# Delta-rule lengths, decays and transposes among projection blocks, norm squares added on VectorE, early modulation rows in fours, gate steps ahead of combines

## The reference, cut to what matters

```python
mod = silu(cond) @ w_ada + b_ada                  # 6 x 1024 values for each of two conditions
h = rmsnorm(x, norm_mix_w) * (1 + sc_a) + sh_a
z = h @ w_in                                      # q, k, v of the four branches, gates
q, k, v = silu(conv(z_q)), silu(conv(z_k)), silu(conv(z_v))      # the delta-rule branch
q, k = l2norm(q), l2norm(k); g = -exp(a_log) * softplus(za + dt_bias); gc = cumsum(g)
o_b = chunked delta rule over (q, k, v, gc, sigmoid(zb)), both directions, * silu(zz)
o_a, o_c, o_d = latent attention, long convolution, differential attention
x = x + gt_a * (sum_n sigmoid(z_gate_n) * (o_n @ w_branch_n)) @ w_out
h = rmsnorm(x, norm_mlp_w) * (1 + sc_m) + sh_m
x = x + gt_m * (relu(h @ w1) ** 2 @ w2)
```

## Time and profile before

| | us |
|---|---|
| median of 3 runs | 3173.61 (3170.78 to 3176.18) |
| the profiled execution, its own time | 3175.59 |
| its span | 3173.6 |
| TensorE busy / VectorE / ScalarE / GpSimd | 93% / 32% / 26% / 21% of the span |
| chain that ended last, by engine | TensorE 87%, VectorE 5%, issue 4%, ScalarE 3%, DMA 1% |

### The profile page before, as it was taken

The page is one execution under the profiler, slowest core; times in us unless marked ns, Lnnn a source line. Parts: engine busy times, 40 slices in busy tenths (PEclk is TensorE's granted clock), DMA queues, the critical chain, the costliest instruction groups (busy, mean ns, idle before and its releaser), DMA issues.

```text
span 3173.6 us, 56302 instructions
## 1 busy us (share of the span) xinstructions
PE 2953.1 (93%) x23304; PEld 2462.0 (78%) x23304; DVE 1022.6 (32%) x1984; ACT 812.6 (26%) x1218; POOL 660.2 (21%) x428
## 2 busy tenths in 40 slices
PE   6998999999999989999999898999999898999997
PEld 3557855777777889999956597567777788999996
DVE  1546613224442121111134374132344322111111
ACT  2123013222322241221231311232222214221222
POOL 0102102111112223333301110021111222333331
PEclk7999999999999999999999899999999999999999
DMA  7110011222113322223230100112221232222222
GB/s 292 34 48 8 3 36 40 77 75 75 61 66 125 111 66 90 85 92 93 93 123 27 34 3 11 51 47 75 75 71 65 84 125 83 87 92 89 85 92 73
DMA packets 56615, 234.64 MB, mean 74 GB/s; under 512 B 6624, under 2 KB 6784, under 8 KB 55136
## 3 DMA queue, kind: packets, MB, share of 16 engines
q1 hardware_dynamic: 53568, 206.67, 19.7%
q0 software_dynamic: 2848, 25.13, 2.1%
HBM read 222.96 MB, written 8.81 MB: 73 GB/s over the span
## 4 chain that ended last, share of the span: by engine, by line
PE 87%; DVE 5%; issue 4%; ACT 3%; DMA 1%; POOL 0%; SPq 0%; DVEq 0%; POOLq 0%; ACTq 0%
PE ps_dense L734 46%; PE ps_dense L727 14%; PE ps_aux L1293 3%; PE ps_dense L1242 2%; PE ps_dense L1314 2%; PE ps_aux L1039 2%; PE ps_aux L1031 2%; PE ps_aux L1019 2%; PE ps_dense L769 1%; PE ps_aux L1242 1%; PE ps_aux L756 1%; DMA w_ring<-in_w_early 1%; PE ps_dense L1305 1%; DVE att_s L2392 1%; PE ps_dense L1088 1%
## 5 line engine op out<-in xcount | busy, mean ns | idle before, releaser
L655 POOL TENSOR_TENSOR w_low<-w_ring,w_high 128x1024 fp32r<-128x1024 f32 x208 | 513.0, 2467 | 1090.1 <-ACT w_high L1547 1088.6
L734 PE MATMUL ps_dense<-h_high,w_high 128*128 128x320 f32 x2048 | 495.4, 323 | 55.6 <-DVE rs L2377 21.9
L734 PE MATMUL ps_dense<-h_low,w_high 128*128 128x320 f32 x2048 | 471.9, 312 | 0.0
L734 PE MATMUL ps_dense<-h_high,w_low 128*128 128x320 f32 x2048 | 471.8, 312 | 0.0
L727 PE MATMUL ps_dense<-h_norm,w_ring 128*128 128x512 f32 (+1 forms) x1536 | 432.8, 443 | 15.5 <-ACT h_norm L1568 7.5
L727 PEld LDWEIGHTS ps_dense<-h_norm,w_ring 128*128 128x128 f32 x1536 | 239.1, 195 | 213.7 <-issue 205.8
L734 PEld LDWEIGHTS ps_dense<-h_high,w_high 128*128 128x128 f32 x2048 | 338.6, 191 | 77.4 <-issue 61.0
L1547 ACT ACTIVATE w_high<-w_ring 128x1024 fp32r<-128x1024 f32 x208 | 218.7, 1053 | 540.2 <-PE ps_dense L734 442.8
L734 PEld LDWEIGHTS ps_dense<-h_high,w_low 128*128 128x128 f32 x2048 | 347.5, 191 | 0.0
L734 PEld LDWEIGHTS ps_dense<-h_low,w_high 128*128 128x128 f32 x2048 | 347.3, 190 | 0.0
L734 PE MATMUL ps_dense<-z_high,w_high 128*128 128x320 f32 x1280 | 296.8, 313 | 13.5 <-POOL w_low L655 13.5
(11 more groups left out here) (386 smaller groups left out, 3288.0 us busy)
## 6 DMA issues: line engine op xcount, KB each, us to landing
w_ring<-in_w_mlp SPq DMA_DIRECT2D x128, 512.0 KB, 3.7
w_ring<-in_w_gate SPq DMA_DIRECT2D x64, 640.0 KB, 3.9
w_ring<-in_w_late SPq DMA_DIRECT2D x64, 512.0 KB, 4.6
w_ring<-in_w_early SPq DMA_DIRECT2D x48, 512.0 KB, 3.7
w_ring<-in_w_in SPq DMA_DIRECT2D x48, 512.0 KB, 3.6
w_ring<-in_w_out SPq DMA_DIRECT2D x16, 512.0 KB, 3.6
arena<-in_dft POOLq DMA_DIRECT2D x2, 3264.0 KB, 12.5
par<-in_par POOLq DMA_DIRECT2D x3, 1731.0 KB, 7.4
```

The lines of the kernel that those rows point to most:

```text
L655: g.tensor_tensor(w_low[:, n % 2], ring[:, slot, 0:KC, :], w_high[:, n % 2].bitcast(F32), ALU.subtract).then_inc(w_low_in.sem, 1)
L734: last = mm(psD[:, b, s * 512:s * 512 + HALF], w_[:, par_, k, :], x_[:, k, s * HALF:(s + 1) * HALF], start=k == 0 and x_ is x_high and w_ ...
```

## The change

**Delta rule.** TensorE's list, in units of blocks: before, 8, 9, 10, cumulative sum, 11, length 0, 12, length 1, 13, lengths 2 and 3, all transposes. Now 8, 9, 10, lengths 0 and 1, 11, cumulative sum, lengths 2 and 3, 12, transposes, 13. The transposes use four PSUM banks in turn instead of two. ScalarE's squares come as soon as each silu is there, two Ln before the eviction of block 11 and two behind it, the Exp of the lengths before the decays' Exp, the last tanh behind both, and the evictions of blocks 12 and 13 each with its tanh, 12 before and 13 behind the k and v evictions. VectorE's list follows.

```diff
-                for n in range(8, 11):
-                    win_block(l, n)
...
-                for c in range(4):
-                    if c < 3:
-                        win_block(l, 11 + c)
+                win_block(l, 8)
+                win_block(l, 9)
+                win_block(l, 10)
+                length(0)
+                length(1)
+                win_block(l, 11)
+                pe.wait_ge(*g_ready.nth(l, 1))
+                pe.wait_ge(*qk_ln.nth(l, 2))
...
+                length(2)
+                length(3)
+                win_block(l, 12)
+
                 pe.wait_ge(*qk_norm.nth(l, 1))
                 for t in range(NT):
-                    if t >= 2:
-                        pe.wait_ge(*kv_tok.nth(l, t - 1))
+                    if t >= 4:
+                        pe.wait_ge(*kv_tok.nth(l, t - 3))
...
+                win_block(l, 13)
```

```diff
+            def norm_sum(l, at_end):
+                pe.wait_ge(*squares_in.nth(l, (1 + at_end) * (KC - 2)))
+                for a, b in SEGS:
+                    mm(psD[:, 0, a:b], c_("ones"), h[:, KC - 2, a:b], start=True, stop=False)
+                pe.wait_ge(*x_squared.nth(l, (2 + at_end) * KC))
+                for a, b in SEGS:
+                    last = mm(psD[:, 0, a:b], c_("ones"), h[:, KC - 1, a:b], start=False, stop=True)
...
+            def sum_squares(l, c, at_end):
+
+                n = at_end * (KC - 2) + c
+                dve.wait_ge(*x_squared.nth(l, (1 + at_end) * KC + c + 1))
+                if c > 1:
+                    dve.wait_ge(*squares_in.nth(l, n - 1))
+                v.tensor_tensor(h[:, c], h[:, c], h[:, c - 1], ALU.add).then_inc(squares_in.sem, 1)
...
-                with act.Fori(0, GROUPS - 1) as g:
+                with act.Fori(0, GROUPS - 2) as g:
                     mlp_group(l, g + 1, 0)
+                mlp_group(l, GROUPS - 1, 0, True)
...
             with act.Fori(0, DEPTH) as l:
                 chain.l, chain.n = l, 0
-                norm(l, 0)
+                root(l, 0)
```

```diff
+                at = 2 * (PACK - 1 - j)
                 for k in range(KC):
-                    last = mm(out[32 * (k % 4):32 * (k % 4) + 32], cond_pad[:, k, :], ring[:, slot, k, :],
-                              start=k < 4, stop=k >= 4)
+                    last = mm(out[32 * (k % 4):32 * (k % 4) + 32], cond_pad[:, k, at:at + 32], ring[:, slot, k, :],
+                              start=j == 0 and k < 4, stop=j == of - 1 and k >= 4, skip_group_check=True)
```

```diff
                     gate_part(l, 3 * v_ - 2)
                     row_max(v_)
+                    gate_sum(l, 3 * v_ - 2)
+                    gate_part(l, 3 * v_ - 1)
                     combine(v_)
-                    gate_part(l, 3 * v_ - 1)
                     take_values(v_ - 1)
+                    gate_sum(l, 3 * v_ - 1)
                     gate_part(l, 3 * v_)
+                    gate_sum(l, 3 * v_)
```

More of the change, by code:

```diff
@@ L910, in gdn, with length @@
             def gdn(l):
-                for n in range(8, 11):
-                    win_block(l, n)
[L915 to L920, removed]
-                for c in range(4):
-                    if c < 3:
-                        win_block(l, 11 + c)
+                def length(c):
                     pe.wait_ge(*qk_sq.nth(l, c + 1))
-                    if c == 1:
+                    if c == 3:
                         pe.wait_ge(*cum_in.nth(l, 1))
@@ L1517, in _ @@
                 pe.wait_ge(*residual.nth(l, 7))
+                norm_sum(l, 0)
+                mlp(l)
+                pe.wait_ge(*residual.nth(l, 39))
                 norm_sum(l, 1)
-                mlp(l)
-                norm_sum(l + 1, 0)
         @block.scalar
@@ L1547, in high_part, with square, squares, root @@
                 a(w_high[:, n % 2], ring[:, j, 0:KC, :], ACT.Copy).then_inc(w_high_in.sem, 1)
-            def norm(l, which):
+            def square(l, c, n):
+                act.wait_ge(*residual.nth(l, n))
+                a(h[:, c], x[:, c], ACT.Square).then_inc(x_squared.sem, 1)
+            def squares(l):
                 for c in range(KC):
-                    if which and c + 2 < N_OUT:
+                    if c + 2 < N_OUT:
                         high_part(l, B_OUT + c + 2, c + 2)
[L1553 to L1558, removed]
+                    square(l, c, c + 1)
+                mlp_high(l, 0, 0)
+                mlp_high(l, 1, 0)
+            def root(l, which):
                 act.wait_ge(*sumsq_done.nth(l, which + 1))
@@ L1642, in gdn, with gate_in @@
                 a(f8("es"), f8("es"), ACT.Exp).then_inc(cum_exp.sem, 1)
-                length_ln(l, 2)
-                length_ln(l, 3)
-                act.wait_ge(*qk_ln.nth(l, 4))
-                a(rn, rn, ACT.Exp, scale=-0.5).then_inc(qk_rs.sem, 1)
-                for c in range(2):
+                silu_tanh(l, 5)
+                def gate_in(c):
+                    act.wait_ge(*block_done.nth(l, 12 + c + 1))
+                    a(gz[:, c], psD[:, c, 0:T], ACT.Copy).then_inc(dense_out.sem, 1)
                     act.wait_ge(*dense_out.nth(l, 13 + c))
@@ L1891, in _ @@
             act.wait_ge(const_in.sem, 16)
+            for c in range(KC):
+                square(0, c, 0)
             with act.Fori(0, DEPTH) as l:
                 chain.l, chain.n = l, 0
-                norm(l, 0)
+                root(l, 0)
                 modulate(l, 0)
@@ L1902, in _ @@
                 high_part(l, B_OUT + 1, 1, 0, 3)
-                norm(l, 1)
+                squares(l)
+                root(l, 1)
                 modulate(l, 1)
@@ L1908, in _ @@
             chain.l, chain.n = DEPTH, 0
-            norm(DEPTH, 0)
+            root(DEPTH, 0)
             for c in range(KC):
```

197 lines of the change are left out of this document (117 added, 80 removed).

## The result

| | us |
|---|---|
| changed kernel, median of 4 runs | 3098.29 (3091.97 to 3102.03) |
| kernel before, median of 4 runs | 3173.23 (3170.78 to 3176.18) |
| ratio, 95% interval | 0.9762 (0.9745 to 0.9778) |
| span of the profiled execution | 3098.9 (before 3173.6) |

Forecast were 3094.0 us and a range of 3082 to 3114. The measured time lies 4.3 us above the forecast, inside the range. The sum hides larger errors of both signs, though. To see them I cut both timelines of TensorE at the same events and compared the stages: length, idle time of TensorE in them, and time that went missing to the clock (the sum of 1 minus the granted clock over stretches of 1 us).

What follows compares the result with a forecast made beforehand. TensorE, busy 2953.1 of 3173.6 us, was taken as the bound. Start 5.2, delta rule 30.2, attention 20.2, norms 18.5 and MLP 5.5 sum to 79.6; 3175.6 becomes 3096.0, less 2.0 as median: 3094.0 us, range 3082 to 3114.

Steps and rivals of the forecast that it cites:

- Delta rule: Before the scan: reordered lengths, block 12 and transposes start the scan 14.1 us earlier in layer 0, 16.1 in layer 1; -30.2 us.
- Start: At the kernel's start: of 16 turns taking 6.99 us, four are left, 1.75 us; -5.2 us.
- Attention: Attention steps: gate product or kept-rows copy ahead of `combine` shortens TensorE's waits, 11.0 plus 9.2 us; -20.2 us.
- Norms: Four norms: six of eight pairs of TensorE products go, the gain smaller where ScalarE is last; -18.5 us.
- Middle: Middle norm of each layer: Ln can start 3.4 us earlier, twice, 6.9 us.
- Between the layers: Norm between layers: Ln starts 3.9 us earlier, not 7.75, because ScalarE's branch stands before the table load.
- Last norm: Norm at the end: only the last square comes after the last residual, so Ln starts 7.75 us earlier.
- MLP turns: MLP: 12 of 16 turns go in each layer, 24 x 0.23 us; -5.5 us.
- moved waits: Rival, attention: `turn` waits for `combine`, so the waits move and 20.2 us are lost; 3114 us, chance 0.08.
- longer chain: Rival, delta rule: the lengths' chain is longer, TensorE waits 4 to 5 us more per layer before transposes; 3103, chance 0.10.
- free branch: Rival, between layers: ScalarE's branch costs nothing, 3.9 us more are gained; 3090 us, chance 0.07.

## Why the prediction was right, and where it was not

- **Start.** -4.93 against -5.2. Right.
- **Delta rule.** Order, cover and wait as laid out; -14.10 and -13.88. For layer 1 I had added 1.7 us for the scan's first matmuls, and they do take 2.05 instead of 3.78; but the stage behind lost as much to the clock as before (6.8), and only 0.7 was kept. In layer 0 it lost 2.9 more and cost 1.46. In layer 1 the low clock came later instead of not at all: before, it lasted from 1797.7 to 1811.4 us, over the scan's start; now it is low for 3.4 us from 1766.6 on, 10 us behind that start.
- **Attention.** The waits fell by 10.2 us in each layer, 10.1 forecast, and `turn` never came to wait for `combine`. The step that failed is one that the prediction did not have: it priced each wait at its own length. The lengths fell by 8.8 us more than the waits, because the clock no longer fell four times in each layer; the run with the product alone ahead shows it.
- **Norms.** Middle -3.15 and -2.95 against -3.4. Between the layers the length from the last MLP product on fell by 4.5 (16.33 to 11.79, forecast 3.9; the branch was 3.26, not 4.3), shown by the run with the last square behind the branch. Last norm -7.6 against -7.75.
- **MLP turns.** Nearly right, though the gaps hide it. From the first MLP product to the last it was 471.23 us before and 468.71 with 140 instructions of padding, where no gap is left: 2.5 us for the 12 turns of a layer, 0.21 us each, 5.1 us in all against 5.5. The rows before show it too. Without the turn the next two products would start at 1150.60 and 1150.89. They start at 1150.74 and 1151.12, so the second is 0.23 us late:

```profile
1150.60 0.28 PE L763 MATMUL ps_aux<-con,rows_kept 128*128 128x2 f32 x2
1150.74 0.54 PE L734 MATMUL ps_dense<-h_high,w_high 128*128 128x320 f32 x2
1151.12 0.46 PE L734 MATMUL ps_dense<-h_low,w_high 128*128 128x320 f32 x2
```

- **What was missing.** Nowhere did I ask where TensorE's own loops lie. I had looked at branches on ScalarE and VectorE, and wrote of TensorE's at the layer's end that it is covered. The MLP loop's cost 10.0 us in six seams, 8.4 of them idle, as padding showed in both kernels.

So 79.6 forecast, less 10.0 for the seams, 0.5 for the turns, 2.4 for the scan stages and 1.0 for the start, the norms and the rest, plus 9.0 in the attention, are the 74.7 by which the span fell. Two omissions of 9 and 10 us cancelled: that the sum came within 4.3 us of the measurement is in part luck. The rivals of moved waits, of a longer chain and of a free branch are refuted by the rows above.

What stays open: why the scan stages of the same code take from 284.7 to 292.5 us in the executions profiled here. Their idle time is the same, 18.7, and the length follows the clock (2.9 lost in the shortest, 11.9 in the longest), but what decides the clock there was not tried.

## What to carry to other kernels

When a change adds or removes instructions ahead of a large loop, compare the packets of that engine's instruction queue before and after: a jump by a whole number per pass (here 9, six times) says that the loop's code no longer stays, and the gap at the seam may be put down to an innocent semaphore. Price a wait on TensorE together with the clock behind it, from rows on both sides of it. And look what every engine does just after a loop's branch; the branch belongs into the engine's idle time, in front of its last wait and not behind it.

## What the runs showed of the hardware that was not expected

- The place of a loop of about 1,700 TensorE instructions changed the time of the same work by 5 us in 470. With 40 instructions of padding there were twelve gaps instead of six, the longest 2.0 us, and the products took 479.1 and 480.1 us.
- A do-nothing instruction with a semaphore count took TensorE 0.147 us: as filler it is free only where the engine idles anyway.
- Around the branch to the top of a layer 3.26 us went by on ScalarE with nothing waited for. On VectorE it was 4.31 us before and 2.48 after, so the price is not a constant.
- In a period of 55 us, a wait of 1.98 us and one of 1.37 us were followed by some 3.4 us at 1.2 GHz, which cost 1.3 us each time. Without the longer wait all four of each layer were gone, without the shorter one two of four.
